# A two-layer decoder trunk on one core: x and the memory loaded feature-major, the first weight unit in halves, sums of squares from the feature-major tiles

## The chip, the core and the metric

The kernel runs on one core of a Trainium2 chip. The time is the device time of one execution in microseconds (us), the median of three runs. The engines are PE (TensorE, matrix products; PEld its weight loads), DVE (VectorE), ACT (ScalarE), POOL (GpSimd) and SP (SyncE, which here only issues transfers). ACT issues transfers too.

## The reference, cut to what matters

```python
def rmsnorm(x, g):
    xf = x.astype(jnp.float32)
    y = xf * lax.rsqrt(jnp.mean(xf * xf, axis=-1, keepdims=True) + EPS)
    return (y * g.astype(jnp.float32)).astype(x.dtype)

# x (1, 512, 1024), mem (1, 256, 1024), all float32; two layers
# layer 0 mixer: z = rmsnorm(x) @ w_in; pooling over windows 2/4/8/16 and spatial gating; @ w_out
# layer 1 mixer: z = rmsnorm(x) @ w_in; dilated attention and retention; @ w_out
# each layer then:
#   cross attention (4 heads) of rmsnorm(x) into rmsnorm(mem): kv = mem_n @ wkv, ... @ wo, added to x
#   SwiGLU: (silu(g) * u) @ w_down with g, u = rmsnorm(x) @ w_gate_up, added to x
# a final rmsnorm ends it
```

The change touches only what comes first: the load of `x` and `mem`, the first two normalisations (of `mem` for layer 0's cross attention, of `x` for layer 0's mixer), and the key and value projection of `mem` (`mem_n @ wkv`).

## The kernel before, in words

Activations are held feature-major: features on the 128 partitions in 8 tiles (`KT`), tokens along the free axis (512 of `x` in `hT`, 256 of `mem` in `memT`). Every product is made of three passes (`three`, L1328): each operand is split in a high part, rounded to the engine's fp32r, and a low part, the rest, and high times high, high times low and low times high are added in PSUM.

The weights come as 256 "units" of 128 x 1024 floats (512 KB) through a ring of four slots. For unit n, SP issues the transfer into `raw` (L415, L420) as soon as the low part of unit n-4 has been made, ACT makes `w_hi` (`split`, L438) once unit n-4 has been used by PE, DVE makes `w_lo` (L824) from both, and PE uses the unit. ACT and DVE make unit n+3 (`LEAD`) in the part of their programs that belongs to unit n. Each engine's program is written out in its own block (`block.sync`, `scalar`, `gpsimd`, `vector`, `tensor`) and runs in the order in which it stands; only semaphores tie them together. PSUM has four accumulators `accs` and four small ones `auxs`, each used in turn; `aux_plan` lists who uses an `aux` in which order, and `acc_free(t)` lets PE start output tile t only when tile t-4 has been drained by DVE.

The start of the program:

- `mem` and `x` come token-major, as the reference has them, into `mem_tok` and `x_tok`. PE turns them with the identity matrix (L1437 for `mem`, `turn_x`, L1445, for `x`), DVE copies the turned memory out of PSUM (L928), ACT the turned `x` (L507).
- Key rows: units 0 to 7 times `mem_hi`/`mem_lo` (256 tokens), one output tile a unit (`rows_unit`). For unit 0, PE waits before each k for `mlo_ready`, the low part of memory tile k. After unit 2 PE spreads `rstd_m` over a tile (L1459, "mem row"); DVE needs that copy, `rstd_mrow` (L944), before it can drain the first key tile (`kv_drain`, L912), and PE needs that drain before unit 4.
- Value columns: units 8 to 15 (`cols_units`), in two groups of four units with two output tiles (tokens on partitions) a group. `turn_x` stands before each group. DVE drains the tiles with `kv_drain` (L915).
- The mixer's V: units 16 to 19 into four output tiles. Its first four tiles need those four accumulators, so its third tile needs the drain of the second group's first tile.
- Beside the value columns ACT makes for each feature tile j of `x` the copy `hT` (L507) and `u_hi` (L509), DVE `u_lo` (`u_lo_part`, L832).
- Sums of squares: ACT takes them along the tokens' rows with an accumulating Square of `mem_tok` (L481) and of `x_tok` (L496). DVE makes the variance (L938, L958), POOL the power -1/2 (`power`, L738). From the second normalisation on it is done otherwise: ACT squares the feature-major tiles (`residual`, L447), POOL adds the eight squares (`add_squares`, L751), PE multiplies the sum with a column of 1/D (`mean`, L1390) and DVE adds epsilon (`mean_to_var`, L850).
- ACT issues five loads of constants (L497 to L501) ahead of the high part of unit 11.

Of the kernel before, what the change touches and what calls it, by code (L numbers as in the profile page):

```python
# [41 lines left out]
P = 128  # L42
D = 1024
# [49 lines left out]
def aux_plan():  # L93
# [7 lines left out]
    add("mem", "vvvv")  # L101
    add("mem row", "v")
    add("x", "a" * 8)
# [51 lines left out]
def program(nc, d):  # L155
    who, aux_at = aux_plan()

    with ExitStack() as ctx:
# [17 lines left out]
        x_tok = at("x_tok", 0, [P, TT, D])  # L176
        mem_tok = at("mem_tok", 56, [P, MT, D])
# [54 lines left out]
        ssq = fixed("ssq", [P, TT])  # L232
        ssq_m = fixed("ssq_m", [P, MT])
# [31 lines left out]
        x_in = sem("x_in")  # L265
# [6 lines left out]
        x_sq = sem("x_sq")  # L272
# [128 lines left out]
        mem_rows = d["mem"].rearrange("a (t p) n -> p (a t) n", p=P)  # L401
# [27 lines left out]
        def _(act):  # L429
# [10 lines left out]
            def residual(norm, j, gcol, t):  # L440
# [11 lines left out]
            def mem_hi_part(layer, j):  # L452
                act.wait_ge(aux_free_v, freed_v(aux_at["mem"] + j // 2))
# [63 lines left out]
            for t in range(TT):  # L517
# [4 lines left out]
                if t == 0:  # L522
                    act.wait_ge(x_sq, TT + MT)
# [207 lines left out]
        def _(pool):  # L731
# [78 lines left out]
        def _(dve):  # L810
# [114 lines left out]
            for t in range(4):  # L925
# [929 lines left out]
```

## Time and profile before

| what | us |
|---|---|
| median of 3 runs (lowest, highest) | 1461.34 (1461.01, 1462.16) |
| span of the profiled execution, first to last instruction | 1459.4 |
| PE busy in it | 1438.1 |
| first product of the kernel starts at | 13.37 |
| last product's stretch begins (closing sums and output) | 1446.3 |

The profiled execution has no time of its own beside its span; the median of the runs is 1.9 us above that span, for what lies around it. A row of a timeline gives start, length, engine, line, operation, result and operands; "idle before" is how long that engine had nothing, and what ended it. A length holds the end of one instruction that overlaps the start of the next, so the pace of a sequence is taken from start to start.

### The profile page before, as it was taken

What the parts mean: (1) busy time and instruction counts of PE and PEld (TensorE: products, weight loads), DVE (VectorE), ACT (ScalarE), POOL (GpSimd) and SP (SyncE); (2) the same over time, 40 slices, a digit from 0 to 9 for tenths busy, and PEclk for the clock granted to TensorE, in tenths of its full rate; (3) what the DMA queues carried; (4) which work ended last, traced back from release to release, by engine and by line L of the source; (5) the groups of instructions that cost most, each with busy time, mean ns of one, the idle gap of its engine ahead of it and who ended that gap; (6) DMA issues with size and microseconds to landing.
All of it is one profiled execution on the core that took longest, in us unless ns stands there. A gap on an engine that the chain in (4) does not pass through costs nothing.

```text
span 1459.4 us, 17837 instructions
## 1 busy us (share of the span) xinstructions
PE 1438.1 (99%) x6738; PEld 1187.7 (81%) x6738; DVE 733.1 (50%) x1030; ACT 529.0 (36%) x794; POOL 105.7 (7%) x89
## 2 busy tenths in 40 slices
PE   7999999999999999999999999999999999999997
PEld 7888888888888888888876778988888888888885
DVE  6746456444444443334567656755545444443331
ACT  6633444332332222223644513534433223222221
POOL 0012200100000000000201101100020000000000
PEclk9999999999999999999999999999999999999999
DMA  7522320222223223233221121442132322223221
GB/s 265 201 74 85 103 98 32 94 94 101 89 97 101 96 99 108 102 105 125 96 73 58 58 73 57 163 158 85 44 116 87 101 89 98 101 95 107 101 73 57
DMA packets 41032, 144.34 MB, mean 99 GB/s; under 512 B 4752, under 2 KB 5904, under 8 KB 40976
## 3 DMA queue, kind: packets, MB, share of 16 engines
q1 hardware_dynamic: 37984, 136.86, 27.7%
q10 hardware_dynamic: 2992, 6.69, 1.3%
q8 instruction: 41, 0.67, 0.2%
q14 instruction: 15, 0.12, 0.0%
HBM read 141.43 MB, written 2.10 MB: 98 GB/s over the span
## 4 chain that ended last, share of the span: by engine, by line
PE 96%; DVE 2%; ACT 1%; DMA 0%; POOL 0%; issue 0%; ACTq 0%; POOLq 0%
PE acc L1330 27%; PE acc L1331 27%; PE acc L1332 27%; PE acc L1373 3%; PE acc L1375 2%; PE acc L1374 2%; PE aux L1635 1%; PE acc L1660 1%; PE aux L1648 1%; DMA mem_tok<-in_mem 0%; PE aux L1332 0%; PE aux L1331 0%; PE aux L1330 0%; DVE xpt_lo L1057 0%; DVE xp L1074 0%; PE aux L1671 0%
## 5 line engine op out<-in xcount | busy, mean ns | idle before, releaser
L824 DVE TENSOR_TENSOR w_lo<-raw,w_hi 128x1024 fp32r<-128x1024 f32 x256 | 316.0, 1235 | 346.8 <-ACT w_hi L438 346.5
L1330 PE MATMUL acc<-u_hi,w_hi 128*128 128x512 f32 x1056 | 413.1, 391 | 0.0
L1332 PE MATMUL acc<-u_hi,w_lo 128*128 128x512 f32 x1056 | 411.0, 389 | 0.0
L1331 PE MATMUL acc<-u_lo,w_hi 128*128 128x512 f32 x1056 | 411.0, 389 | 0.0
L438 ACT ACTIVATE w_hi<-raw 128x1024 fp32r<-128x1024 f32 x256 | 269.2, 1053 | 388.4 <-DVE tmp L1149 192.1
L1332 PEld LDWEIGHTS acc<-u_hi,w_lo 128*128 128x128 f32 x1056 | 198.2, 188 | 41.6
L1330 PEld LDWEIGHTS acc<-u_hi,w_hi 128*128 128x128 f32 x1056 | 198.2, 188 | 41.1 <-issue 0.5
L1331 PEld LDWEIGHTS acc<-u_lo,w_hi 128*128 128x128 f32 x1056 | 198.3, 188 | 40.2
L1330 PE MATMUL acc<-act_hi,w_hi 128*128 128x512 f32 x352 | 137.5, 391 | 0.0
L1332 PE MATMUL acc<-act_hi,w_lo 128*128 128x512 f32 x352 | 137.1, 389 | 0.0
L1331 PE MATMUL acc<-act_lo,w_hi 128*128 128x512 f32 x352 | 137.0, 389 | 0.0
L751 POOL TENSOR_TENSOR sqsum<-sqsum,tmp 128x512 f32<-128x512 f32 x42 | 54.4, 1296 | 1019.7 <-ACT tmp L447 1019.7
L1330 PE MATMUL acc<-y_hi,w_hi 128*128 128x512 f32 x256 | 100.0, 391 | 0.0
L1332 PE MATMUL acc<-y_hi,w_lo 128*128 128x512 f32 x256 | 99.6, 389 | 0.0
L1331 PE MATMUL acc<-y_lo,w_hi 128*128 128x512 f32 x256 | 99.6, 389 | 0.0
L1332 PEld LDWEIGHTS acc<-act_hi,w_lo 128*128 128x128 f32 x352 | 66.1, 188 | 13.9
L1331 PEld LDWEIGHTS acc<-act_lo,w_hi 128*128 128x128 f32 x352 | 66.1, 188 | 13.5
L1330 PEld LDWEIGHTS acc<-act_hi,w_hi 128*128 128x128 f32 x352 | 66.1, 188 | 13.5
L622 ACT ACTIVATE tmp<-tmp 128x512 f32<-128x512 f32 x44 | 27.8, 632 | 133.4 <-DVE tmp L1137 133.4
L447 ACT ACTIVATE tmp<-hT 128x512 f32<-128x512 f32 x42 | 26.6, 633 | 134.6 <-DVE hT L896 134.6
L1145 DVE TENSOR_TENSOR tmp<-acc,rstd_row 128x512 f32<-128x512 f32 x44 | 30.4, 691 | 78.8 <-PE acc L1332 78.8
L896 DVE TENSOR_TENSOR hT<-hT,acc 128x512 f32<-128x512 f32 x48 | 32.9, 685 | 73.3 <-PE acc L1332 73.3
(172 smaller groups left out, 1615.5 us busy)
## 6 DMA issues: line engine op xcount, KB each, us to landing
raw<-in_weights SPq DMA_DIRECT2D x256, 512.0 KB, 3.4
x_tok<-in_x ACTq DMA_DIRECT2D x4, 512.0 KB, 6.0
out_h<-y_tok SPq DMA_DIRECT2D x4, 512.0 KB, 3.9
decay<-in_decay ACTq DMA_DIRECT2D x1, 768.0 KB, 4.9
mem_tok<-in_mem SPq DMA_DIRECT2D x2, 256.0 KB, 3.6
mem_tok<-in_mem ACTq DMA_DIRECT2D x2, 256.0 KB, 6.5
cs_d<-in_cs_d ACTq DMA_DIRECT2D x1, 512.0 KB, 3.5
cs_r<-in_cs_r ACTq DMA_DIRECT2D x1, 512.0 KB, 4.4
```

Of the source, the lines that this page charges most:

```text
L438: act.activation(w_hi[:, s, :], raw[:, s, :], ACT.Copy).then_inc(hi_ready, 1)
L622: act.activation(tmp[:, e, :], tmp[:, e, :], ACT.Silu).then_inc(silu_ready, 1)
L751: pool.tensor_tensor(sqsum[:, :], sqsum[:, :], tmp[:, j % 2, :], ALU.add).then_inc(sq_added, 1)
L824: dve.tensor_tensor(w_lo[:, s, :], raw[:, s, :], w_hi[:, s, :].bitcast(F32), ALU.subtract)\
L896: dve.tensor_tensor(hT[:, j, :], hT[:, j, :], acc(a0 + j)[:, :], ALU.add).then_inc(acc_drained, 1)
L1145: dve.tensor_tensor(tmp[:, 2 + e, :], acc(tg + 1)[:, :], rstd_row[:, :], ALU.mult)\
L1330: pe.matmul(out, w_h, x_h, start=first, stop=False)
L1331: pe.matmul(out, w_h, x_l, start=False, stop=False)
L1332: return pe.matmul(out, w_l, x_h, start=False, stop=last)
L1373: pe.matmul(out, x_h[:, k, tok], w_hi[:, s, w], start=(k == 0), stop=False)
L1374: pe.matmul(out, x_h[:, k, tok], w_lo[:, s, w], start=False, stop=False)
L1375: ins = pe.matmul(out, x_l[:, k, tok], w_hi[:, s, w], start=False, stop=(k == KT - 1))
```

## The change

Before the program starts, `x` and `mem` are laid out feature-major, so that the loads go straight into `hT` and `memT` and nothing is turned. SP issues memory quarter 0, the first half of unit 0, quarter 1, the second half of unit 0, quarters 2 and 3, and then units 1 to 3 without waiting; ACT loads `vecs` first. ACT and DVE make the first half of unit 0 as a piece of its own, and PE starts on it (`first_lo`), waiting for the second half at k = 4. The memory's squares and their sum are made by POOL (eight tensor_tensor instructions), PE takes the mean after unit 2, and "mem row" stands after unit 3 in place of after unit 2. `x` comes in four parts, issued by ACT during the key rows. Its squares are made by ACT in place of the `hT` copies, POOL adds them (`add_squares(0)`), and `mean(0)` and `row(0)` stand after the first and second unit of V, where `row(0)` stood after the sixth unit of the value columns.

```diff
-    add("mem", "vvvv")
+    add("mem mean", "v")
     add("mem row", "v")
-    add("x", "a" * 8)
+    add(("mean", 0), "v")
     add(("row", 0), "v")
...
         @block.sync
         def _(sp):
-            for q in (0, 2):
-                sp.dma_start(mem_tok[:, :, q * 256:(q + 1) * 256], mem_rows[:, :, q * 256:(q + 1) * 256])\
-                    .then_inc(mem_in[q], 16)
-            for j in range(RING):
-                if j == 1:
-
-                    for q in range(4):
-                        sp.wait_ge(mem_in[q], 16)
+            def mem_part(q):
+                sp.dma_start(memT[:, 2 * q:2 * q + 2, :], d["mem_t"][:, 2 * q:2 * q + 2, :]).then_inc(mem_in[q], 16)
+
+            mem_part(0)
+            sp.dma_start(raw[:, 0, 0:UW // 2], d["weights"][0, :, 0:UW // 2]).then_inc(first_in, 16)
+            mem_part(1)
+            sp.dma_start(raw[:, 0, UW // 2:UW], d["weights"][0, :, UW // 2:UW]).then_inc(raw_in[0], 16)
+            mem_part(2)
+            mem_part(3)
+            for j in range(1, RING):
                 sp.dma_start(raw[:, j, :], d["weights"][j]).then_inc(raw_in[j], 16)
...
+            act.dma_start(vecs[:, :], d["vecs"]).then_inc(vecs_in, 16)
             act.dma_start(ident[:, :], d["ident"]).then_inc(ident_in, 16)
...
+            act.activation(warm[:, :], vecs[:, 0:1], ACT.Copy)
+            mem_hi_part(0, 0)
+            mem_hi_part(0, 1)
+            act.wait_ge(first_in, 16)
+            act.activation(w_hi[:, 0, 0:UW // 2], raw[:, 0, 0:UW // 2], ACT.Copy).then_inc(first_hi, 1)
+            mem_hi_part(0, 2)
+            mem_hi_part(0, 3)
+            act.wait_ge(raw_in[0], 16)
+            act.activation(w_hi[:, 0, UW // 2:UW], raw[:, 0, UW // 2:UW], ACT.Copy).then_inc(hi_ready, 1)
+            for j in range(4, KT):
                 mem_hi_part(0, j)
             for n in range(1, LEAD):
                 split(n)
-            for t in range(MT):
-                if t:
-                    act.wait_ge(x_sq, t)
-                act.activation(junk, mem_tok[:, t, :], ACT.Square, accum_out=ssq_m[:, t:t + 1]).then_inc(x_sq, 1)
-            for t in range(TT):
-                act.dma_start(x_tok[:, t, :], d["x"][0, t * P:(t + 1) * P, :]).then_inc(x_in, 16)
             for j in range(KT):
                 split(j + LEAD)
+                if j in (1, 3, 5, 7):
+                    q = j // 2
+                    act.dma_start(hT[:, 2 * q:2 * q + 2, :], d["x_t"][:, 2 * q:2 * q + 2, :]).then_inc(x_in[q], 16)
...
-                t = j - (KT - TT)
-                if t >= 0:
-                    act.wait_ge(x_in, 16 * TT)
-
-                    act.wait_ge(x_sq, MT + t)
-                    act.activation(junk, x_tok[:, t, :], ACT.Square, accum_out=ssq[:, t:t + 1]).then_inc(x_sq, 1)
...
-                act.activation(hT[:, j, :], auxs[t % 4][:, :], ACT.Copy).then_inc(aux_free_a, 1)
-                act.wait_ge(aux_free_a, freed_a(t))
+                act.wait_ge(x_in[j // 2], 16)
+                if j >= 3:
+                    act.wait_ge(sq_added, j - 2)
+                act.activation(sqsum[:, :] if j == 0 else tmp[:, j % 2, :], hT[:, j, :], ACT.Square)\
+                    .then_inc(sq_ready, 1)
...
-            pool.wait_ge(var_ready, 1)
+            for q in range(4):
+                pool.wait_ge(mem_in[q], 16)
+                pool.tensor_tensor(mem_sq[:, min(q, 1), :, :], memT[:, 2 * q:2 * q + 2, :], memT[:, 2 * q:2 * q + 2, :],
+                                   ALU.mult).then_inc(mem_squared, 1)
+                pool.wait_ge(mem_squared, max(2 * q, 1))
+                if q:
+                    pool.tensor_tensor(mem_sq[:, 0, :, :], mem_sq[:, 0, :, :], mem_sq[:, 1, :, :], ALU.add)\
+                        .then_inc(mem_squared, 1)
+                    pool.wait_ge(mem_squared, 2 * q + 1)
+            pool.tensor_tensor(mem_sq[:, 0, 0, :], mem_sq[:, 0, 0, :], mem_sq[:, 0, 1, :], ALU.add)\
+                .then_inc(mem_squared, 1)
+            pool.wait_ge(aux_free_v, freed_v(aux_at["mem mean"]))
             power(rstd_m[:, :], var_m[:, :], MT)
-            pool.wait_ge(var_ready, 2)
-            power(rstd_tok[:, :], var_e[:, :], TT)
+            add_squares(0)
+            norm_power(0)
...
             for j in range(KT):
                 split(j + LEAD)
+                if j == 1:
+                    t = aux_at["mem mean"]
+                    dve.wait_ge(aux_done, t + 1)
+                    dve.tensor_scalar(var_m[:, :], auxs[t % 4][:, 0:MT], EPS, None, ALU.add).then_inc(aux_free_v, 1)
...
                 if j == 2:
+                    t = aux_at["mem mean"]
+                    pe.wait_ge(mem_squared, 8)
+                    pe.wait_ge(const_set, 3)
+                    for m in range(MT):
+                        ins = pe.matmul(auxs[t % 4][:, m:m + 1], mem_sq[:, 0, 0, m * P:(m + 1) * P], mean_w[:, :],
+                                        start=True, stop=True)
+                    ins.then_inc(aux_done, 1)
+                if j == 3:
...
-            pe.wait_ge(x_in, 16 * TT)
-            for j in range(4):
-                turn_x(j)
             cols_units(u0 + KT, a0 + A_XV, mem_hi, mem_lo, MT)
-            for j in range(4, 8):
-                turn_x(j)
-            cols_units(u0 + KT + 4, a0 + A_XV + 2, mem_hi, mem_lo, MT, after=lambda q: row(0) if q == 1 else None)
+            cols_units(u0 + KT + 4, a0 + A_XV + 2, mem_hi, mem_lo, MT)
...
-            cols_units(u0 + U_V, a0 + A_V, u_hi, u_lo, TT, before=u_in(0))
+            cols_units(u0 + U_V, a0 + A_V, u_hi, u_lo, TT, before=u_in(0), after=stats_after(0))
```

What stands on two engines before and after, with the semaphores that each row waits for. First DVE at the start of the program, before (`memT` is the turned memory, L824 makes a weight unit's low part, L876 a memory tile's):

```order
L928 COPY memT<-aux 128x512 [waits aux_done] x3
L824 TENSOR_TENSOR w_lo<-raw,w_hi 128x1024 [waits hi_ready]
L928 COPY memT<-aux 128x512 [waits aux_done]
L876 SCALAR_TENSOR_TENSOR mem_lo<-memT,vecs,mem_hi 128x256 [waits mhi_ready,aux_free_v]
L876 SCALAR_TENSOR_TENSOR mem_lo<-memT,vecs,mem_hi 128x256 [waits mhi_ready] x7
L824 TENSOR_TENSOR w_lo<-raw,w_hi 128x1024 [waits hi_ready] x2
L938 TENSOR_SCALAR var_m<-ssq_m 128x2 [waits x_sq]
L824 TENSOR_TENSOR w_lo<-raw,w_hi 128x1024 [waits hi_ready] x3
L944 COPY rstd_mrow<-aux 128x256 [waits aux_done]
```

And DVE at the same place after the change:

```order
L885 SCALAR_TENSOR_TENSOR mem_lo<-memT,vecs,mem_hi 128x256 [waits mhi_ready] x2
L937 TENSOR_TENSOR w_lo<-raw,w_hi 128x512 [waits first_hi]
L885 SCALAR_TENSOR_TENSOR mem_lo<-memT,vecs,mem_hi 128x256 [waits mhi_ready] x2
L942 TENSOR_TENSOR w_lo<-raw,w_hi 128x512 [waits hi_ready]
L885 SCALAR_TENSOR_TENSOR mem_lo<-memT,vecs,mem_hi 128x256 [waits mhi_ready] x4
L833 TENSOR_TENSOR w_lo<-raw,w_hi 128x1024 [waits hi_ready] x4
L953 TENSOR_SCALAR var_m<-aux 128x2 [waits aux_done]
L833 TENSOR_TENSOR w_lo<-raw,w_hi 128x1024 [waits hi_ready]
L957 COPY rstd_mrow<-aux 128x256 [waits aux_done]
```

The copies are gone, the low parts of the memory's tiles and of unit 0 alternate, and the variance of the memory now waits for PE (`aux_done`). POOL from the start of the program to the mixer, before:

```order
L738 TENSOR_TENSOR rstd_m<-var_m,mexp 128x2 [waits var_ready,const_set]
L738 TENSOR_TENSOR rstd_tok<-var_e,mexp 128x4 [waits var_ready]
L759 AFFINE_SELECT ws_t<-ws_t 128x512 [waits c0_in]
L738 TENSOR_TENSOR rstd_v<-var_v,mexp 128x4 [waits var_ready,acc_drained]
L780 TENSOR_TENSOR wsum<-a_pad 128x527
```

And POOL after the change (`mem_sq` holds the memory's squares, `sqsum` the sum of x's):

```order
L753 TENSOR_TENSOR mem_sq<-memT 128x512 [waits mem_in0,const_set]
L753 TENSOR_TENSOR mem_sq<-memT 128x512 [waits mem_in1,mem_squared]
L757 TENSOR_TENSOR mem_sq<-mem_sq 128x512 [waits mem_squared]
L753 TENSOR_TENSOR mem_sq<-memT 128x512 [waits mem_in2,mem_squared]
L757 TENSOR_TENSOR mem_sq<-mem_sq 128x512 [waits mem_squared]
L753 TENSOR_TENSOR mem_sq<-memT 128x512 [waits mem_in3,mem_squared]
L757 TENSOR_TENSOR mem_sq<-mem_sq 128x512 [waits mem_squared]
L760 TENSOR_TENSOR mem_sq<-mem_sq 128x256 [waits mem_squared]
L736 TENSOR_TENSOR rstd_m<-var_m,mexp 128x2 [waits aux_free_v]
L749 TENSOR_TENSOR sqsum<-sqsum,tmp 128x512 [waits sq_ready]
L749 TENSOR_TENSOR sqsum<-sqsum,tmp 128x512 [waits sq_added,sq_ready] x6
L736 TENSOR_TENSOR rstd_tok<-var_e,mexp 128x4 [waits aux_free_v]
```

POOL had three instructions on four columns or fewer and one on 512 up to the mixer's pooling; it now has 15 more on whole tiles, eight at the start of the program and seven beside the value columns.

## Rows read from the trace of the kernel before

**Rows 1.** Section 1 of the page: busy us (share of the span) xinstructions.

```profile
PE 1438.1 (99%) x6738; PEld 1187.7 (81%) x6738; DVE 733.1 (50%) x1030; ACT 529.0 (36%) x794; POOL 105.7 (7%) x89
```

**Rows 2.** Chain of waits up to the first product: start us, us, what.

```profile
1.83 6.40 DMA mem_tok<-in_mem
...
13.37 0.55 PE acc L1330
```

**Rows 3.** PE by stretch: us, busy (xinstructions), granted clock, DMA share, GB/s.

```profile
13.37:18.84 5.47, 5.47 (x25) 1.00 0.66 225
18.84:24.43 5.59, 5.59 (x48) 1.00 1.01 405
```

**Rows 4.** Timeline of ACT and DVE at the start: start us, us, instruction.

```profile
7.57 0.91 ACT L454 ACTIVATE mem_hi<-memT,vecs 128x256 fp32r<-128x256 f32 x2
...
13.55 1.99 ACT L438 ACTIVATE w_hi<-raw 128x1024 fp32r<-128x1024 f32 x2
...
12.74 3.26 DVE L876 SCALAR_TENSOR_TENSOR mem_lo<-memT,vecs,mem_hi 128x256 fp32r<-128x256 f32 x8
...
15.91 2.36 DVE L824 TENSOR_TENSOR w_lo<-raw,w_hi 128x1024 fp32r<-128x1024 f32 x2
```

**Rows 5.** DMA issues of the page: KB each, us from issue to landing.

```profile
mem_tok<-in_mem SPq DMA_DIRECT2D x2, 256.0 KB, 3.6
```

**Rows 6.** Timeline, POOL and DVE at the same time, three places.

```profile
182.47 1.30 POOL L751 TENSOR_TENSOR sqsum<-sqsum,tmp 128x512 f32<-128x512 f32 x1 [2.79 <-ACT tmp L447]
...
181.64 0.74 DVE L832 SCALAR_TENSOR_TENSOR u_lo<-hT,vecs,u_hi 128x512 fp32r<-128x512 f32 x1
183.04 1.27 DVE L832 SCALAR_TENSOR_TENSOR u_lo<-hT,vecs,u_hi 128x512 fp32r<-128x512 f32 x1 [0.65 <-ACT u_hi L449]
...
103.59 1.33 POOL L780 TENSOR_TENSOR wsum<-a_pad 128x527 f32<-128x527 f32 x1
...
102.45 3.68 DVE L1000 SCALAR_TENSOR_TENSOR vn<-vn,rstd_v,sgu_g 128x512 f32<-128x512 f32 x3 [0.30 <-POOL rstd_v L738]
...
118.88 1.06 POOL L780 TENSOR_TENSOR wsum<-wsum 128x525 f32<-128x525 f32 x1
...
119.59 0.69 DVE L862 TENSOR_TENSOR uu<-acc,rstd_row 128x512 f32<-128x512 f32 x1 [1.71 <-PE acc L1332]
```

**Rows 7.** Timeline of PE where x is turned, and at a later mean.

```profile
39.14 1.91 PE L1445 MATMUL aux<-ident,x_tok 128*128 128x128 f32 x16
...
41.11 0.39 PE L1374 MATMUL acc<-w_lo,mem_hi 128*128 128x512 f32 x1
...
186.25 0.95 PE L1390 MATMUL aux<-mean_w,sqsum 128*128 128x1 f32 x8
...
187.38 0.40 PE L1331 MATMUL acc<-u_lo,w_hi 128*128 128x512 f32 x1
```

**Rows 8.** Timeline of DVE after "mem row".

```profile
26.32 0.41 DVE L944 COPY rstd_mrow<-aux 128x256 f32<-128x256 f32 x1
26.77 0.75 DVE L912 TENSOR_TENSOR xk<-acc,rstd_mrow 128x256 f32<-128x256 f32 x2
```

**Rows 9.** Value columns, 41.04 to 65.36 us: DVE's groups, busy us, mean ns.

```profile
L824 DVE TENSOR_TENSOR w_lo<-raw,w_hi 128x1024 fp32r<-128x1024 f32 x8 | 9.8, 1224 | 7.7 <-ACT w_hi L438 7.7
L832 DVE SCALAR_TENSOR_TENSOR u_lo<-hT,vecs,u_hi 128x512 fp32r<-128x512 f32 x7 | 5.6, 798 | 0.0
L915 DVE TENSOR_SCALAR xv<-acc,rstd_m 128x512 f32<-128x512 f32 x2 | 1.4, 742 | 0.0
L921 DVE TENSOR_TENSOR xv_lo<-xv,xv_hi 128x512 fp32r<-128x512 f32 x2 | 1.3, 682 | 0.0
```

**Rows 10.** Timeline there: ACT's first weight unit, and V's third tile.

```profile
41.32 1.06 ACT L438 ACTIVATE w_hi<-raw 128x1024 fp32r<-128x1024 f32 x1 [2.40 <-issue]
...
64.93 0.39 PE L1373 MATMUL acc<-w_hi,u_hi 128*128 128x512 f32 x1
...
66.29 0.40 PE L1373 MATMUL acc<-w_hi,u_hi 128*128 128x512 f32 x1
```

More of the change, by code:

```diff
@@ L264, in program @@
         vecs_in = sem("vecs_in")
-        x_in = sem("x_in")
+        x_in = [sem(f"x_in{q}") for q in range(4)]
+        first_in = sem("first_in")
+        first_hi = sem("first_hi")
+        first_lo = sem("first_lo")
+        mem_squared = sem("mem_squared")
         c0_in = sem("c0_in")
@@ L522, in _ @@
                 if t == 0:
-                    act.wait_ge(x_sq, TT + MT)
+                    act.wait_ge(sq_added, KT - 1)
                 else:
@@ L746, in add_squares @@
                 for j in range(1, KT):
-                    n = (KT - 1) * (norm - 1) + j
-                    pool.wait_ge(sq_ready, 8 * (norm - 1) + j + 1)
+                    n = (KT - 1) * norm + j
+                    pool.wait_ge(sq_ready, 8 * norm + j + 1)
                     if j > 1:
@@ L765, in _ @@
                 if g == 0:
-                    pool.wait_ge(var_ready, 3)
+                    pool.wait_ge(var_ready, 1)
                     power(rstd_v[:, :], var_v[:, :], TT)
@@ L922, in kv_lo_parts @@
                                       kv_tile(j, xk_hi, xv_hi).bitcast(F32), ALU.subtract).then_inc(kvlo_ready, 1)
-            for t in range(4):
-                k = aux_at["mem"] + t
-                dve.wait_ge(aux_done, k + 1)
-                dve.tensor_copy(memT[:, 2 * t:2 * t + 2, :], auxs[k % 4][:, :].rearrange("p (a b) -> p a b", a=2))\
-                    .then_inc(aux_free_v, 1)
-                if t == 2:
-                    split(0)
-            dve.wait_ge(aux_free_v, freed_v(aux_at["mem"] + 3))
-            for j in range(KT):
+            mem_lo_part(0, 0)
+            mem_lo_part(0, 1)
+            dve.wait_ge(first_hi, 1)
+            dve.tensor_tensor(w_lo[:, 0, 0:UW // 2], raw[:, 0, 0:UW // 2], w_hi[:, 0, 0:UW // 2].bitcast(F32),
+                              ALU.subtract).then_inc(first_lo, 1)
+            mem_lo_part(0, 2)
+            mem_lo_part(0, 3)
+            dve.wait_ge(hi_ready, 1)
+            dve.tensor_tensor(w_lo[:, 0, UW // 2:UW], raw[:, 0, UW // 2:UW], w_hi[:, 0, UW // 2:UW].bitcast(F32),
+                              ALU.subtract).then_inc(lo_ready, 1)
+            for j in range(4, KT):
                 mem_lo_part(0, j)
@@ L936, in _ @@
                 split(n)
-            dve.wait_ge(x_sq, MT)
-            dve.tensor_scalar(var_m[:, :], ssq_m[:, :], 1.0 / D, EPS, ALU.mult, ALU.add).then_inc(var_ready, 1)
             for j in range(KT):
                 split(j + LEAD)
+                if j == 1:
+                    t = aux_at["mem mean"]
+                    dve.wait_ge(aux_done, t + 1)
+                    dve.tensor_scalar(var_m[:, :], auxs[t % 4][:, 0:MT], EPS, None, ALU.add).then_inc(aux_free_v, 1)
                 if j == 2:
@@ L955, in _ @@
                 kv_lo_parts(0, KT + j)
-                if j == 1:
-                    dve.wait_ge(x_sq, MT + TT)
-                    dve.tensor_scalar(var_e[:, 0:TT], ssq[:, 0:TT], 1.0 / D, EPS, ALU.mult, ALU.add)\
-                        .then_inc(var_ready, 1)
                 if j:
@@ L972, in _ @@
                 if n == 0:
+                    mean_to_var(0)
+                if n == 1:
                     make_row(0)
@@ L1345, in rows_unit @@
                 s = n % RING
-                weights_in(n, i)
+                if n == 0:
+                    pe.wait_ge(first_lo, 1)
+                else:
+                    weights_in(n, i)
                 if k0 == 0:
@@ L1349, in rows_unit @@
                 for k in range(kn):
+                    if n == 0 and k == KT // 2:
+                        weights_in(0)
                     if before is not None:
@@ L1425, in kv_proj @@
                     cols_units(u0 + KT + 4 * c, a0 + A_XV + 2 * c, mem_hi, mem_lo, MT)
-            pe.wait_ge(ident_in, 16)
-            for t in range(4):
-                pe.wait_ge(mem_in[t], 16)
-                k = aux_at["mem"] + t
-                aux_free(pe, k)
-                for e in range(2):
-                    for m in range(MT):
-                        c = e * M + m * P
-                        j = 2 * t + e
-                        ins = pe.transpose(auxs[k % 4][:, c:c + P], mem_tok[:, m, j * P:(j + 1) * P], ident[:, :])
-                ins.then_inc(aux_done, 1)
-            def turn_x(j):
-                t = aux_at["x"] + j
-                aux_free(pe, t)
-                for i in range(TT):
-                    ins = pe.transpose(auxs[t % 4][:, i * P:(i + 1) * P], x_tok[:, i, j * P:(j + 1) * P], ident[:, :])
-                ins.then_inc(aux_done, 1)
             a0, u0 = KV_ACC[0], KV_UNIT[0]
@@ L1457, in _ @@
                     pe.wait_ge(rstd_ready, 1)
+                    pe.wait_ge(ident_in, 16)
                     for m in range(MT):
@@ L1835 @@
     arrays = dict(constants())
-    arrays["x"] = np.ascontiguousarray(w["x"])
-    arrays["mem"] = np.ascontiguousarray(w["mem"])
+    arrays["x_t"] = np.ascontiguousarray(w["x"][0].reshape(S, KT, P).transpose(2, 1, 0))
+    arrays["mem_t"] = np.ascontiguousarray(w["mem"][0].reshape(M, KT, P).transpose(2, 1, 0))
     arrays["weights"] = weight_units(w)
```

23 lines of the change are left out of this document (5 added, 18 removed).

## The prediction

> **What bounds the kernel now.** I read the page's busy times first: PE is at work for 1438.1 of 1459.4 us [rows 1], so a change pays only where PE stands still or does work that can go. The chain of waits then shows the largest stop. The memory's turned quarters arrive at 1.83 + 6.40 = 8.23, and the first product starts at 13.37 [rows 2]. The stretches come next. From 13.37 to 18.84 PE begins 25 products in 5.47 us, one each 0.219; from 18.84 to 24.43 it begins 48 in 5.59, one each 0.116 [rows 3]. The granted-clock column reads 1.00 in both, so I go by the spacing: 256 columns in 0.213 us are the lower level, 1.2 GHz, and PE leaves it after 5.5 us of unbroken work. Last I read who is beside whom on DVE and POOL, because the change gives POOL fifteen large instructions in the first 65 us.
>
> **The start.** Added up without POOL it looks like this. A 256 KB load of the memory lands 3.6 us after its issue [rows 5]; quarter 0 is issued at about 0.8 as before, so ACT has it at 4.4 at the latest and I take 4.2, since only `vecs` and `ident` compete with it. Then two `mem_hi` (0.41 each from start to start, 0.91 for two), half a `w_hi` (about 0.55, half of 1.99 / 2), half a `w_lo` (about 0.6, a quarter of 2.36) [rows 4] and some 0.4 for the hand-overs between engines: the first product at 6.5 to 7.0 in place of 13.37, a saving of 6.4.
>
> But DVE pays beside POOL [rows 6]. A `u_lo` that takes 0.74 alone took 1.27 when it started 0.57 after a POOL add: it ended as if it had started when POOL's add was 1.10 old. At 102.45 three DVE instructions of that kind took 3.68, where three in a row need 3 x 0.74 less two overlaps of 0.08, 2.06; two POOL instructions ran in between, and the second took 1.33 where its kind takes 1.06. So the two engines take turns, DVE loses 0.8 to 1.1 for each POOL instruction, and a DVE queue that is full doesn't keep POOL out. The Trainium skill (SBUF — State Buffer, "SBUF: two separate sides") states it as a rule: a DVE instruction with two SBUF inputs and a GpSimd instruction that reads SBUF lock the shared port pair for the whole instruction. The trace agrees, with those 1.27 and 3.68 us.
>
> `mem_lo` and `w_lo` have two SBUF inputs; POOL's eight new instructions (four squares, three adds, half an add) start with the quarter's landing at 4.2, before DVE's first. They cost DVE 4 x 0.95 for the squares (between 0.8 and 1.1), 3 x 1.1 and 0.6, 7.7 in all. DVE's own work to the low part of unit 1 is 8 x 0.40 + 2 x 0.6 + 1.15 = 5.55 [rows 4]. All alternate up to the eighth, so unit 1 is ready at 4.2 + 7.7 + 5.55 = 17.45, and PE starts it at 17.5. Before it started at 13.37 + 24 x 0.213 = 18.5. The start is worth **-1.0**, not -6.4: PE begins unit 0 at about 8.7 but then waits for its tiles. The bounds are -6.4 (POOL costs nothing) and -0.4 (squares at 1.1, one more gap).
>
> The clock: PE's work is broken by those waits until the second half of unit 0 and tile 4 are ready at about 14.4. With 5.5 us of unbroken work as before, the fast spacing begins at 19.9, so 2.4 us of unit 1 run at 0.213 in place of 0.12, **+0.9** after taking off the 0.15 that unit 1 lost before (0 if the broken work counts; +1.9 if the rise comes 2 us later).
>
> **Key rows.** The mean of the memory on PE has two products; the four of a later mean cost from 186.25 + 0.23 to 187.38, 0.9 [rows 7], so **+0.45**. Its wait for POOL's eighth instruction (done at 15) is over by then (24.3). "Mem row" now stands directly ahead of unit 4, and unit 4 needs the first drain, which needs the copy of that row. DVE's wait for the mean stands ahead of unit 5's low part, the copy and the drains; that is in time, since unit 3 (2.9 us) lies between. But nothing covers the copy (0.41), the drain (0.42) and three hand-overs: PE stands **+1.1** [rows 8]. Before, unit 3 covered it. Bounds 0.8 and 2.0, the latter if POOL's power is held up by unit 5's low part.
>
> **x.** The 32 turns go: 41.11 - 39.14 - 0.23 = 1.74 each half [rows 7], **-3.5**. `mean(0)` is four products, **+0.9**; `row(0)` only moves. The loads of x, 2 MB, are issued by ACT at four places in the key rows and needed in the value columns, at least 8 us later than they land; they press on the weights less than before, where they went out together. The squares (ACT) take the place of the `hT` copies of 0.58, and SP's early loads keep weights ahead of PE.
>
> **Value columns.** POOL now adds seven times here, one in each PE unit of 2.72. Let T be PE's start of the value columns. ACT's first `w_hi` there comes at 41.32 [rows 10], 2.2 after the last key unit (39.14), because ACT is still issuing the constants' loads ("issue"); the turns covered that and no longer do, so DVE's first `w_lo` is at T + 3.2. V's third tile needs the drain of the tile that ends at T + 21.8, and is wanted 1.36 later (66.29 - 64.93) [rows 10], at T + 23.1. Up to the end of that drain DVE has 8 `w_lo` at 1.15, 7 `u_lo` at 0.66, 3 drains at 0.66, 2 `xv_lo` at 0.60 and one small tile of 0.35, 17.3 [rows 9] (their mean lengths less the overlap of 0.08), 1.1 of waiting for ACT near the start, and seven POOL adds at 1.1, 7.7: T + 3.2 + 17.3 + 1.1 + 7.7 = T + 29.3. PE stands 6.2. The two drains inside it read PSUM, and one such was not lengthened (0.69 beside POOL's 1.06) [rows 6], so an add may hide beside them: down to 5.1. I take **+5.6**. Without POOL's adds DVE is done at T + 22.7 and nothing stands; so the bounds are 0 and 6.2. Behind that, V's other three units (5.4 each) let DVE catch up, and the later stages keep their margins.
> [...]
>
> **Sum.** -1.0 + 0.9 + 0.45 + 1.1 - 3.5 + 0.9 + 5.6 = +4.45. The span goes from 1459.4 to 1463.9, and the median, 1.9 above it, from 1461.34 to **1465.8**.
>
> **Rivals.**
> - *POOL costs DVE nothing here.* The rows that show the turns are few, and squares with one tile as both inputs might not hold the port. Then the sum is -6.4 + 0.45 + 1.1 - 3.5 + 0.9 = -7.45: 1453.9. Against it stand three places [rows 6].
> - *POOL costs at the start alone.* The adds fall beside drains or in DVE's idle time, or ACT's loads of constants are issued faster than in 4 us, and V's third tile waits 0 to 2: the sum is -1.15 plus about 1, so 1461.2. For it: before, DVE idled 7.7 us in the value columns [rows 9]. Against it: that idling ended with ACT's `w_hi`, once a unit, and in each unit POOL's add becomes ready just as DVE has its two large instructions, 1.15 + 0.66 + 1.1 = 2.9 of 2.72.
> - *Worse than forecast.* Early transfers, now nine at once with 1.25 MB ahead of the last memory quarter, land 1 to 2 us later, and PE, stopped before V for over 5 us, returns to the lower level for some 5 us, where a product of 512 columns takes 0.43 in place of 0.23 (twice 0.213): +2.5 and +1.5 bring 1469.8. It decides once a stop lasts as long as those before the first product, where spacing was slow afterwards.
>
> **Chances.** Forecast 0.52, start alone 0.20, nothing 0.19, worse 0.09. What a measurement of this kernel tells from no change is 0.2%, 2.9 us: under 1458.4 is faster, over 1464.3 slower. Of the forecast's 0.52 some 0.09 lies within that bound, and of "start alone" 0.02 lies on each side of it: slower 0.43 + 0.09 + 0.02 = 0.54, same 0.09 + 0.16 = 0.25, faster 0.19 + 0.02 = 0.21. The likeliest's own range is 1463 to 1468.5; to hold 8 in 10 with the bounds of the start and the stall it reaches from 1454.5 to 1469.
>
> **What would show it.** Right: PE's first product at 8 to 9, but unit 1's not before 17; `mem_lo` of 1.2 to 1.5 us in place of 0.48 beside POOL's squares; PE idle about 1 us at unit 4 and over 4 us at V's third tile, released by DVE's drain; no L1445 rows. Wrong: `mem_lo` at 0.48 beside POOL, unit 1 at 12, no idle time of PE before V. Then the time is near 1454 and the first rival holds.

## The result and the profile after

The changed kernel takes 1466.52 us (median of 5 runs, 1465.86 to 1466.75), the kernel before 1461.34 (1460.52 to 1462.4): ratio 1.0035, 95% interval 1.0024 to 1.0045. It is slower by 5.2 us. The profiled execution is the fastest of the five (1465.86); the spans of the others are 1464.2 to 1465.0. Section 1 of the page, as in [rows 1]:

```profile
span 1464.1 us, 17773 instructions
PE 1437.3 (98%) x6702; PEld 1185.5 (81%) x6702; DVE 743.4 (51%) x1027; ACT 522.6 (36%) x784; POOL 127.3 (9%) x104
```

PE has 36 instructions less and is busy 0.8 us less, yet the span is 4.7 longer. DVE is busy 10.3 us longer with three instructions fewer: some of its rows have become longer, as the timelines below show. The waits of PE up to 90 us (engine, line, released by: us in total, times, longest):

```profile
PE acc L1341 <- DVE w_lo L937: 6.8, 1, 6.8
PE acc L1389 <- DVE xv L924: 4.2, 1, 4.2
PE acc L1341 <- DVE mem_lo L885: 2.7, 3, 1.9
PE acc L1341 <- DVE xk L921: 1.1, 1, 1.1
```

The first is the start, which was 13.37 long [rows 2]; the other three are new. The next fence is the timeline of PE (start us, us, instruction, idle time before it and its releaser) at the first product, the first product of unit 1, the mean of the memory, unit 4, the first value column, V's third tile and the mean of x:

```profile
6.76 0.58 PE L1341 MATMUL acc<-mem_hi,w_hi 128*128 128x256 f32 x1 [6.76 <-DVE w_lo L937]
...
16.81 0.58 PE L1341 MATMUL acc<-mem_hi,w_hi 128*128 128x256 f32 x1
...
24.16 0.50 PE L1453 MATMUL aux<-mean_w,mem_sq 128*128 128x1 f32 x4
...
28.93 0.36 PE L1341 MATMUL acc<-mem_hi,w_hi 128*128 128x256 f32 x1 [1.07 <-DVE xk L921]
...
40.52 0.40 PE L1389 MATMUL acc<-w_hi,mem_hi 128*128 128x512 f32 x1
...
68.06 0.80 PE L1389 MATMUL acc<-w_hi,u_hi 128*128 128x512 f32 x1 [4.24 <-DVE xv L924]
...
73.85 0.94 PE L1406 MATMUL aux<-mean_w,sqsum 128*128 128x1 f32 x8
```

DVE and POOL at the start stand against [rows 4]. POOL's first five rows, and DVE's rows beside them:

```profile
4.39 1.04 POOL L753 TENSOR_TENSOR mem_sq<-memT 128x512 f32<-128x512 f32 x1 [3.36 <-DMA memT<-in_mem_t]
6.16 1.45 POOL L753 TENSOR_TENSOR mem_sq<-memT 128x512 f32<-128x512 f32 x1 [0.73 <-DMA memT<-in_mem_t]
7.69 1.35 POOL L757 TENSOR_TENSOR mem_sq<-mem_sq 128x512 f32<-128x512 f32 x1
9.11 1.10 POOL L753 TENSOR_TENSOR mem_sq<-memT 128x512 f32<-128x512 f32 x1
10.29 1.59 POOL L757 TENSOR_TENSOR mem_sq<-mem_sq 128x512 f32<-128x512 f32 x1
```

```profile
5.09 1.02 DVE L885 SCALAR_TENSOR_TENSOR mem_lo<-memT,vecs,mem_hi 128x256 fp32r<-128x256 f32 x2 [5.09 <-ACT mem_hi L456]
6.03 0.68 DVE L937 TENSOR_TENSOR w_lo<-raw,w_hi 128x512 fp32r<-128x512 f32 x1
6.63 2.68 DVE L885 SCALAR_TENSOR_TENSOR mem_lo<-memT,vecs,mem_hi 128x256 fp32r<-128x256 f32 x2
9.24 1.52 DVE L942 TENSOR_TENSOR w_lo<-raw,w_hi 128x512 fp32r<-128x512 f32 x1
10.68 4.94 DVE L885 SCALAR_TENSOR_TENSOR mem_lo<-memT,vecs,mem_hi 128x256 fp32r<-128x256 f32 x4
```

The first two `mem_lo` take 1.02: POOL's first square ends 0.34 after they begin, and then POOL waits for its DMA. The next two take 2.68; half a `w_lo` takes 0.68 and then 1.52. The value columns look the same. All seven of POOL's adds are there, and in them seven of DVE's rows are 1.04 to 1.10 too long. Shown are three of these rows, a `u_lo` without an add, and the drain that ends the stop:

```profile
45.76 1.78 DVE L841 SCALAR_TENSOR_TENSOR u_lo<-hT,vecs,u_hi 128x512 fp32r<-128x512 f32 x1
...
55.68 2.38 DVE L930 TENSOR_TENSOR xv_lo<-xv,xv_hi 128x512 fp32r<-128x512 f32 x2
...
62.58 2.31 DVE L833 TENSOR_TENSOR w_lo<-raw,w_hi 128x1024 fp32r<-128x1024 f32 x1
64.81 0.74 DVE L841 SCALAR_TENSOR_TENSOR u_lo<-hT,vecs,u_hi 128x512 fp32r<-128x512 f32 x1
...
67.27 1.40 DVE L924 TENSOR_SCALAR xv<-acc,rstd_m 128x512 f32<-128x512 f32 x2
```

The first `u_lo` takes 1.78 beside an add, and 0.74 once the last add has ended (at 63.80). What the stop leaves behind shows in PE by stretch (from:to and length in us, PE busy (xinstructions), then PEld, DVE, ACT and POOL in the same way, granted clock, DMA share, GB/s):

```profile
63.66:68.06 4.40, 0.17 (x2) 0.00 (x1) 4.40 (x6) 0.02 (x1) 0.14 (x1) 1.00 0.42 148
68.06:71.56 3.50, 3.50 (x8) 2.79 (x9) 3.50 (x5) 2.19 (x3) 0.00 (x0) 0.51 0.44 142
71.56:73.85 2.29, 2.29 (x11) 1.88 (x10) 0.10 (x1) 0.00 (x0) 0.00 (x0) 1.00 0.44 111
```

After 4.24 us of idle time the granted clock is 0.51, the 1.2 GHz level, and eight products take 3.50 us. Later products of V start 0.227 apart, so eight would take 1.8. The stop costs 4.24 + 1.7 = 5.9.

### The profile page after: what moved, and what is told of

It reads as the page before. It is cut to its first block, busy times and chain, and to the rows that moved or that the text cites. A ratio compares the mean times of both kernels' runs of the same rounds, so it can differ in the third digit from the quotient of the medians.

```text
span 1464.1 us, 17773 instructions
## 1 busy us (share of the span) xinstructions
PE 1437.3 (98%) x6702; PEld 1185.5 (81%) x6702; DVE 743.4 (51%) x1027; ACT 522.6 (36%) x784; POOL 127.3 (9%) x104
## 3 DMA queue, kind: packets, MB, share of 16 engines
q10 hardware_dynamic: 2448, 6.16, 1.3%
## 4 chain that ended last, share of the span: by engine, by line
PE 93%; DVE 4%; ACT 1%; POOL 0%; ACTq 0%; DMA 0%; issue 0%; POOLq 0%
PE acc L1341 27%; PE acc L1343 27%; PE acc L1342 27%; PE acc L1389 2%; PE acc L1390 2%; PE acc L1391 2%; PE aux L1635 1%; PE acc L1660 1%; DVE w_lo L833 1%; DVE u_lo L841 1%; PE aux L1648 1%; DVE mem_lo L885 1%; PE aux L1343 0%; PE aux L1342 0%; PE aux L1341 0%; DVE xpt_lo L1068 0%
## 5 line engine op out<-in xcount | busy, mean ns | idle before, releaser
L749 POOL TENSOR_TENSOR sqsum<-sqsum,tmp 128x512 f32<-128x512 f32 x49 | 66.6, 1359 | 1044.6 <-ACT tmp L449 1019.4
```

What stands on the lines that cost most here:

```text
L749: pool.tensor_tensor(sqsum[:, :], sqsum[:, :], tmp[:, j % 2, :], ALU.add).then_inc(sq_added, 1)
```

## The experiments

Each median is of 5 or 11 executions. The kernel before took 1461.05 to 1461.2 us beside them. In this table "V's third tile" is PE's idle time ahead of it, and "slow after" says that products at the 1.2 GHz level followed it. "Unit 4 at" gives the start of that unit; "no stop" says that PE did not wait ahead of it.

| run | us | ratio to before, 95% | unit 4 at | V's third tile |
|---|---|---|---|---|
| changed kernel | 1466.52 | 1.0024 to 1.0045 | 28.93 | 4.24, slow after |
| e1 memory sums out | 1461.26 | 0.9991 to 1.0009 | 22.53 | 5.38, slow after |
| e2 x adds out | 1459.94 | 0.9984 to 1.0002 | 29.06 | none |
| e3 both out | 1454.20 | 0.9939 to 0.9966 | 22.81 | none |
| e4 POOL writes only | 1455.35 | 0.9951 to 0.9978 | 24.49 | none |
| e5 e1, row earlier | 1459.38 | 0.9979 to 0.9997 | 21.73, no stop | 4.42, slow after |
| e6 unit 0 whole | 1467.88 | 1.0031 to 1.0059 | 30.32 | 4.36, slow after |
| e7 before, with adds | 1462.48 | 0.9999 to 1.0017 | 27.03, no stop | 0.91 |
| e9 adds on VectorE | 1462.91 | 1.0003 to 1.0021 | 29.51 | 1.94 |
| e8 sums moved | 1452.34 | 0.9926 to 0.9954 | 21.48, no stop | none |

**e1, e2, e3: take POOL's two burdens away, one and both.** In e1:

```diff
-            for q in range(4):
-                pool.wait_ge(mem_in[q], 16)
-                pool.tensor_tensor(mem_sq[:, min(q, 1), :, :], memT[:, 2 * q:2 * q + 2, :], memT[:, 2 * q:2 * q + 2, :],
...
+            pool.memset(mem_sq[:, 0, 0, :], 1.0).then_inc(mem_squared, 8)
```

In e2 (and e3 has both edits):

```diff
-                    pool.tensor_tensor(sqsum[:, :], sqsum[:, :], tmp[:, j % 2, :], ALU.add).then_inc(sq_added, 1)
+                    if norm == 0:
+                        pool.memset(spare[:, :], 0.0).then_inc(sq_added, 1)
+                        continue
```

> The changed kernel with the memory's eight POOL instructions left out (the sum of squares is a constant; layer 0's keys and values are scaled wrongly). Theory (POOL and DVE take turns on instructions with two SBUF inputs): mem_lo falls to 0.48 us each, unit 1 starts at 12.4 in place of 16.81 and the fast spacing comes before unit 2, so unit 2 starts at 15.3 in place of 21.28: 6.0 us off, 1460.5. The stop of 4.2 before V's third tile stays. Rival A (the tiles of the memory arrive late, the transfers bound the start): no POOL work changes nothing, 1466.5. Rival B (ACT and DVE slow each other): the same.

> The changed kernel with POOL's seven adds of x's squares left out (the sum holds tile 0 alone, so the first normalisation of x is wrong). Theory: u_lo falls from 1.8 to 0.74, and PE's stop of 4.2 before V's third tile goes: 1462.3. Rival (DVE is late there because ACT, which issues the loads of the constants, starts the value columns 2 us late): at most 1 us goes, 1465.5 or more.

> The changed kernel without either of POOL's two sums (both are constants or tile 0 alone). Theory: the two costs add, 6.0 + 4.2 = 10.2 off 1466.5: 1456.3, which is 5.0 under the kernel before. Rival (they overlap: a start that is earlier by 6 only makes PE wait longer for DVE later): 1460 to 1462.

Measured: 5.3 us less, 6.6 less, and 12.3 less with both, where the two alone add up to 11.8. So both burdens cost, they cost about independently, and everything else in the change is worth 1461.05 - 1454.20 = 6.9 us of gain (e3 does neither sum, so this is not the gain of a complete kernel). DVE's rows at the start in e1:

```profile
6.63 0.88 DVE L875 SCALAR_TENSOR_TENSOR mem_lo<-memT,vecs,mem_hi 128x256 fp32r<-128x256 f32 x2
7.48 0.69 DVE L932 TENSOR_TENSOR w_lo<-raw,w_hi 128x512 fp32r<-128x512 f32 x1
8.14 1.69 DVE L875 SCALAR_TENSOR_TENSOR mem_lo<-memT,vecs,mem_hi 128x256 fp32r<-128x256 f32 x4
```

The same pair of `mem_lo` takes 0.88 in place of 2.68. But PE gains 6.4 us up to unit 4 and keeps less: in e1's profiled execution the stop before V's third tile is 5.38 long, and the slow clock behind it lasts longer:

```profile
63.45:66.90 3.45, 3.45 (x8) 2.77 (x9) 3.45 (x5) 2.19 (x3) 0.00 (x0) 0.50 0.40 141
66.90:70.34 3.44, 3.44 (x11) 2.64 (x11) 0.15 (x1) 0.00 (x0) 0.00 (x0) 0.67 0.48 152
```

So in this execution part of what one end gave was taken at the other. It is the slowest of e1's eleven (1459.6 to 1462.43), and in it ACT came to its first weight unit of the value columns late (see e5), so how much is lost as a rule isn't shown. In e2 PE does the way from the first value column to the mean of x without idle time and at full clock (granted clock 1.00 from start to end):

```profile
40.65:67.94 27.29, 27.29 (x122) 22.46 (x121) 22.19 (x28) 21.06 (x30) 0.69 (x7) 1.00 0.67 231
```

That way took 73.85 - 40.52 = 33.33 in the changed kernel, 6.0 more, which is the 4.24 of idle time and the 1.7 of slow clock. My expectation for e2 (1462.3) had only the idle time in it; the real saving is larger by the clock. e3 came out 2.1 lower than expected, most of it for the same reason.

**e4: POOL as busy, but reading nothing.** Each of the eight squares and sums, and each add, becomes a memset of 2048 columns.

```diff
-                pool.tensor_tensor(mem_sq[:, min(q, 1), :, :], memT[:, 2 * q:2 * q + 2, :], memT[:, 2 * q:2 * q + 2, :],
-                                   ALU.mult).then_inc(mem_squared, 1)
+                pool.memset(filler[:, :], 1.0).then_inc(mem_squared, 1)
```

> The changed kernel with each of POOL's fifteen tile instructions replaced by a memset of 2048 columns, which writes SBUF and reads nothing (both sums are left out). Theory as the Trainium skill has it (only reads by GpSimd meet DVE's second input): as e3, 1456.3, with mem_lo at 0.48. Rival C (any POOL instruction on SBUF holds DVE for its length): 1464 to 1467, mem_lo above 1 us. If the memsets take longer than 1.3 us the wait of PE for the eighth may add some us; the row of mem_lo decides then.

Measured 1455.35 with POOL occupied from 4.70 on:

```profile
4.70 3.67 POOL L759 MEMSET filler<- 128x2048 f32 x2 [3.30 <-DMA memT<-in_mem_t]
8.43 1.80 POOL L762 MEMSET filler<- 128x2048 f32 x1
```

```profile
6.95 0.88 DVE L888 SCALAR_TENSOR_TENSOR mem_lo<-memT,vecs,mem_hi 128x256 fp32r<-128x256 f32 x2
7.87 0.69 DVE L945 TENSOR_TENSOR w_lo<-raw,w_hi 128x512 fp32r<-128x512 f32 x1
```

POOL instructions of 1.80 us, with DVE's rows as short as without them; in the value columns too, where seven memsets run, `u_lo` takes 0.74 to 0.75. What is 1.2 over e3 is in the main one wait: PE's mean stood 1.31 us for the eighth memset. So it isn't that POOL is busy, or that it writes SBUF, that holds DVE here; what the memsets leave out is reading. The Trainium skill (SBUF — State Buffer, "SBUF: two separate sides") confines the lock for a DVE instruction with two SBUF inputs to a GpSimd instruction that reads SBUF; this run agrees, 0.88 against 2.68 us.

**e5: the row of the memory one unit earlier** (e1's edit, and the mean behind unit 1, the row behind unit 2).

```diff
-                if j == 3:
+                if j == 2:
                     t = aux_at["mem row"]
```

> Left out: the GpSimd squares and sums of the memory (the place is filled with a constant, as in the run without the memory's sums). Beside that, the memory's mean goes behind unit 1 instead of unit 2 and its row behind unit 2 instead of unit 3. My theory: the 1.07 us stop of TensorE before unit 4 is the chain from the row product over VectorE's copy and its first drain, which units lying behind it cover; with the row one unit earlier it goes, the four mean and row products cost what they did, and the time is 1.0 to 1.3 us under the run without the memory's sums (1461.26 us), about 1460.1. Rival: VectorE reaches the copy late anyway and the stop only moves before unit 3 or unit 4, with the same length: 1461.3 us.

Measured 1459.38, 1.9 under e1 in place of 1.1. The stop before unit 4 is gone, as expected. The rest lies further on, as far as the two traces tell, which are both of the slowest execution of their run: the stop at V's third tile is 4.42 here and 5.38 in e1, where the constants' loads on ACT's queue were slow, so ACT's next `w_hi` came 2.5 us after the value columns' start. These two timeline rows are from e1:

```profile
35.54 0.97 ACTq L498 DMA_DIRECT2D invcnt<-in_invcnt  x1
36.62 1.06 ACT L440 ACTIVATE w_hi<-raw 128x1024 fp32r<-128x1024 f32 x1 [2.74 <-issue]
```

and this from the changed kernel, whose value columns begin at 40.52, so 0.6 before it:

```profile
41.10 1.06 ACT L440 ACTIVATE w_hi<-raw 128x1024 fp32r<-128x1024 f32 x1 [1.83 <-PE acc L1343]
```

**e6: unit 0 whole again.**

```diff
-            sp.dma_start(raw[:, 0, 0:UW // 2], d["weights"][0, :, 0:UW // 2]).then_inc(first_in, 16)
+            sp.dma_start(raw[:, 0, :], d["weights"][0]).then_inc(raw_in[0], 16)
```

> The changed kernel with one part undone: unit 0 of the weights is loaded, rounded and subtracted whole, as before. My theory: the first product comes about 1 us later (7.5 to 8.5 instead of 6.76) but unit 1 still starts at 16.5 to 17, since what it waits for is VectorE's queue of eight memory rows and two weight units beside GpSimd's eleven instructions, which the halves hardly alter; the time stays within 0.7 us of the changed kernel (1466.5). Rival: the halves' head start is carried through to unit 1, and the time rises by the whole 1 to 1.5 us that the first product loses: 1467.5 to 1468.

Measured 1467.88, 1.4 us more, as the rival had it and not I; but the first product comes at 9.03 (2.3 later), and of that unit 1 keeps 0.8 (17.63). The rest up to 1.4 is products at the low level: at 21.6 they still start 0.21 apart, where the changed kernel's are 0.12 apart from 20.2 on. This rest isn't shown to come from the edit. In e9, whose start is the changed kernel's (first product at 6.82, unit 1 at 16.89), the fast spacing begins at 21.5 and unit 4 at 29.51, 0.6 later than there. The 0.8 goes with a hole in DVE's queue, which the first half fills in the changed kernel:

```profile
7.15 1.82 DVE L829 TENSOR_TENSOR w_lo<-raw,w_hi 128x1024 fp32r<-128x1024 f32 x1 [1.19 <-ACT w_hi L439]
```

Where DVE is what PE waits for, every idle microsecond of DVE before that point counts; I had treated the queue as full from its first row (and POOL's instructions there are eight, not eleven). So the halves earn 0.8 us at unit 1 even beside POOL.

**e7: the kernel before with seven POOL instructions added** in its value columns.

```diff
+            for j in range(1, KT):
+                pool.wait_ge(uhi_ready, j + 1)
+                pool.wait_ge(dummy, j)
+                pool.tensor_tensor(sqsum[:, :], sqsum[:, :], sqsum[:, :], ALU.mult).then_inc(dummy, 1)
```

> The kernel before, with seven GpSimd instructions that it does not have and does not need: products of a 128x512 tile with itself, each started when the next column of u_hi is ready, as the changed kernel's adds are. My theory: each costs VectorE 0.8 to 1.1 us of its own rows in the value columns, 6 to 7 us together; before has some 3 to 4 us of VectorE's idle time there, so its drains come 2 to 4 us late, TensorE stops at V's third tile, and the time is 1463 to 1465. Rival: GpSimd's adds by themselves cost nothing, and what stops the changed kernel there is that its value columns start earlier and in another order: 1461.1 us and no stop.

Measured 1462.48, +1.3, with an interval (0.9999 to 1.0017) that touches no change: by the time alone this run is inconclusive. The trace isn't. Seven of DVE's rows are longer again, and PE has a stop at V's third tile that before hasn't:

```profile
59.37 1.52 DVE L839 SCALAR_TENSOR_TENSOR u_lo<-hT,vecs,u_hi 128x512 fp32r<-128x512 f32 x1
```

```profile
66.77 0.50 PE L1380 MATMUL acc<-w_hi,u_hi 128*128 128x512 f32 x1 [0.91 <-DVE xv L922]
```

The price is less than I expected: 0.78 on a `u_lo` (1.52 - 0.74) and not 1.04. This POOL instruction multiplies one tile with itself, the adds read two tiles. The start of the changed kernel shows the same pair of prices: beside a square of `memT` (POOL at 9.11) half a `w_lo` was 0.83 too long. Whether the second tile or the kind of operation makes the difference wasn't tried. Counted from the first turn of x (38.55 here, 39.14 in before), the drain moved from 26.2 to 27.4 us, so of some 5.4 us of charges (six of 0.78, one of 0.7) 1.2 came through; the rest went into the 7.7 us that DVE idled there [rows 9]. A drain, which reads PSUM, shows no charge: POOL's L766 on 512 columns (65.58, 0.98 long) ran beside the first of two drains, and the two took 1.40 together, as they do without it.

**e9: the same adds on DVE.** The memory's sums stay on POOL.

```diff
-            add_squares(0)
...
                 if j:
                     u_lo_part(0, j - 1, C_EVEN)
+                    add_square(j - 1)
```

> The changed kernel with the seven adds of the x squares on VectorE, each behind the lower half of the same column, instead of on GpSimd; the memory's sums stay as they are. My theory: on GpSimd each add costs exactly one of VectorE's two-input rows 1.04 to 1.10 us (7.4 us for seven in the changed kernel's trace); on VectorE the add itself takes 0.69 us and holds nobody, seven make 4.8. So its drain before V's third tile comes 2.6 us earlier, the stop of 4.24 falls to 1 to 2 us, and the time is 1463 to 1464.5, under the changed kernel's 1466.5 but over 1459.9 without the adds. Rival: the stop follows from how much work is queued before the drain, not from the ports; then VectorE, which now has 4.8 us more to do, is as late or later: 1466.5 to 1471.

Measured 1462.91, 3.6 under the changed kernel. An engine that does seven instructions more is done earlier:

```profile
64.28 0.75 DVE L840 SCALAR_TENSOR_TENSOR u_lo<-hT,vecs,u_hi 128x512 fp32r<-128x512 f32 x1
64.94 0.69 DVE L850 TENSOR_TENSOR sqsum<-sqsum,tmp 128x512 f32<-128x512 f32 x1
```

```profile
66.34 0.50 PE L1398 MATMUL acc<-w_hi,u_hi 128*128 128x512 f32 x1 [1.94 <-DVE xv L931]
```

The stop falls from 4.24 to 1.94, 2.3 in place of the 2.6 worked out; and after it the granted clock stays at 1.00, so the way from V's third tile to the mean of x (66.34 to 70.56) is 1.6 shorter. Of these 3.9 the later start of unit 4 took 0.6 back. My range began at 1463, just above the result. The rival, that the length of the queue alone decides, is out. Against e2, seven adds cost 3.0 us on DVE and 6.6 on POOL.

**e8: everything kept, at other places.** The memory's squares on ACT, their adds on DVE, the mean inside unit 2, the row inside unit 3; the x squares in tiles of their own, and POOL's adds behind the last value drain.

```diff
+            for q in range(4):
+                act.activation(mem_sq[:, q, :, :], memT[:, 2 * q:2 * q + 2, :], ACT.Square).then_inc(mem_squared, 1)
...
-                act.activation(sqsum[:, :] if j == 0 else tmp[:, j % 2, :], hT[:, j, :], ACT.Square)\
-                    .then_inc(sq_ready, 1)
+                act.activation(x_sq[:, j, :], hT[:, j, :], ACT.Square).then_inc(sq_ready, 1)
...
+            pool.wait_ge(acc_drained, KV_ACC[0] + A_XV + 4)
...
+                dve.tensor_tensor(mem_sq[:, 0, :, :], mem_sq[:, 0, :, :], mem_sq[:, q, :, :], ALU.add)\
+                    .then_inc(mem_added, 1)
...
+                    if j == 2 and k == 4:
+                        memory_stats(2)
+                    if j == 3 and k == 3:
+                        memory_stats(3)
```

> The changed kernel with all the sums kept, but at other places: the memory's four squares on ScalarE behind the first five weight units, their four adds on VectorE at the same place, the memory's mean inside unit 2 and its row inside unit 3; the x squares stay in eight tiles of their own, and GpSimd adds them only when VectorE has drained all twelve key and value tiles, with the mean of x behind V's third unit and its row behind the fourth. My theory: both of GpSimd's burdens and the stop before unit 4 go, so it ends 1.1 us below the run that leaves both sums out (1454.2): 1453.1, from 1452.5 to 1454.5. Rival: the squares cost wherever they are done, since ScalarE's four (about 0.7 us each) and VectorE's four adds (1.2 each) delay weight units 5 and 6 or the first keys' drain by 3 us or more: 1456 to 1458; or the late mean of x makes the first products behind V wait: 1455.

Measured 1452.34 (1451.94 to 1452.57), just under the range that I gave: 8.8 us under the kernel before and 14.2 under the changed one. After the start, PE has no stop up to the mean of x. POOL's adds still run, where DVE has slack. All seven, and DVE's rows beside the first of them:

```profile
56.70 4.07 POOL L752 TENSOR_TENSOR sqsum<-x_sq 128x512 f32<-128x512 f32 x1 [37.79 <-DVE xv L917]
60.92 10.05 POOL L752 TENSOR_TENSOR sqsum<-sqsum,x_sq 128x512 f32<-128x512 f32 x6
```

```profile
56.54 0.74 DVE L834 SCALAR_TENSOR_TENSOR u_lo<-hT,vecs,u_hi 128x512 fp32r<-128x512 f32 x1
57.20 1.28 DVE L923 TENSOR_TENSOR xv_lo<-xv,xv_hi 128x512 fp32r<-128x512 f32 x2
58.41 1.22 DVE L826 TENSOR_TENSOR w_lo<-raw,w_hi 128x1024 fp32r<-128x1024 f32 x1
```

Here the two engines don't take turns. Four two-input rows of DVE stand back to back, none is longer than alone, and it is POOL that waits: its add takes 4.07 where most of the others take 1.30, and ends 1.1 us after the last of them. Of the later adds two met a `w_lo`, which took 1.65 and 1.31 in place of 1.22. So seven adds cost DVE 0.5 us here and 7.4 in the changed kernel; why the first add waits here and is let in there wasn't tried.

It is 1.9 under e3, which doesn't make the sums at all; 1.1 of that is the stop before unit 4, and the other 0.8 I haven't taken apart.

## Why the prediction was right

The time forecast was 1465.8 and came out 1466.52; the span forecast was 1463.9 and that of the profiled execution 1464.1. The causes and the direction are as forecast, but the close hit owes something to errors that cancelled. By its steps:

- **The start, -1.0.** Unit 1 starts at 16.81, forecast 17.5. In the kernel before it started at 18.63, not at 18.5 (its first product took 0.35 and not 0.213), so the start gave -1.8. The mechanism holds (e1, e4), but two sizes were off. The first product comes at 6.76 and not at 8 to 9, one of the signs that I had named; unit 1 is just under the 17 of the other. The reason is that memory quarter 1 landed at 6.16: the page now gives a median of 4.8 us from issue to landing for these loads, where I had taken 3.6 from [rows 5]. POOL's second square waited for it, and DVE's first three rows went through nearly uncharged. And six of POOL's eight instructions were charged, 6.1 us in place of 7.7.
- **The clock, +0.9.** The fast spacing begins at 20.2, forecast 19.9. But unit 1 began earlier than forecast, so 3.4 us of it were slow and not 2.4, and the term is +1.5. It took back most of what the start gave beyond its forecast. That the onset came within 0.3 is partly luck, since e9 has it at 21.5 behind the same start. Unit 4 begins at 28.93 and began at 27.61 before: +1.3, where the forecast's first four terms give +1.45.
- **The row of the memory, +1.1.** PE idles 1.07; e5 takes it away.
- **x turns, -3.5, and the mean, +0.9.** No L1445 rows are left. The change without both burdens gains 6.9 (e3), where the first rival's sum had 7.45.
- **V's third tile, +5.6.** The total is right (5.9), its parts aren't. The stop is 4.24: the drain comes at T + 27.5, not T + 29.3, because the constants' loads took 2.7 us on ACT's queue (38.31 to 40.99) and not 4.2, and ACT was at T + 0.6 in place of T + 2.2. All seven adds were charged, at 1.04 to 1.10. The 0.6 that I took off for an add beside a drain didn't come into play: no add of this trace runs beside one. And 1.7 is the slow clock after the stop. I had this mechanism in the rival "worse than forecast", with "over 5 us" as the point from which it decides; it set in at 4.24. Two errors of 1.4 and 1.7 with opposite signs cancelled, and that was luck.
- **POOL against DVE.** "Costs at the start alone" is out through e2 (6.6 us), "costs nothing" through e1 and e2, "the work and not the reads" through e4.

The prediction also says that a full queue of DVE doesn't keep POOL out. That held wherever the two met in the changed kernel, but not in e8, where POOL's add stood 2.9 us behind four rows of DVE.

What stays open: how long the slow clock lasts after a stop. From V's third tile to the mean of x, e9 took 4.22 us (66.34 to 70.56, at full clock), the changed kernel 5.79, e1 6.89 and e5 7.10 (60.97 to 68.07), after stops of 1.94, 4.24, 5.38 and 4.42: not in the order of the stops.

## What to carry to other kernels

Work that is given to GpSimd because it is idle can be paid for by VectorE, where a GpSimd instruction reads SBUF tiles beside VectorE instructions with two SBUF inputs. As an estimate from these traces, count up to one VectorE delay of 0.8 to 1.1 us for each instruction of 512 columns (the changed kernel and e7 paid that, e8 much less), and compare it with doing the work on VectorE itself (0.69 us here). So ask first whether VectorE is what the matmuls wait for in that stretch; if it is, put the work on ScalarE, or behind the last drain, and a change that lost 5 us gains 9 with the same sums. And a stop of TensorE can cost more than its length: here those of 4.24 to 5.38 us had slow products behind them, those of 0.91 and 1.94 had none.

## What was unexpected

- A stop of 4.24 us was followed by eight products at 1.2 GHz (granted clock 0.51, one each 0.43 us in place of 0.227); one of 1.94 us by none. At the start of the program the granted-clock column read 1.00 while the products of 256 columns were 0.213 apart, so there only the spacing tells the level.
- The memory's 256 KB loads took 4.8 us from issue to landing (median of four) in place of 3.6 (the two on SP's queue before). The first of them still landed 3.6 after its issue (0.81, POOL began on it at 4.39), and the two that the kernel before issued on ACT's queue had taken 6.5. That the transfers ahead of them are the cause is likely but wasn't tried.
- The fast spacing began at 20.2 in the changed kernel and at 21.5 in e9, with the same products before it to within 0.1 us. So half a microsecond between two single traces need not be the work of an edit.
- The same five constants' loads took 2.7 us to issue from ACT's queue in one kernel and 3.6 in another (e1: 32.92 to 36.51) that differs only in what GpSimd does at the start.
